# Key rope rotated on GpSimd, and the key-value latent turned ahead of the fourth query product, in a two-layer encoder

## What is computed

```python
def _mla(h, pos, w_in, g_q, g_kv, w_uq, w_ukv, w_o):
    lat = h @ w_in
    cq, ckv, k_rope = jnp.split(lat, [Q_LORA, Q_LORA + KV_LORA], axis=-1)      # 384, 256, 32
    cq = _rmsnorm(cq, g_q)
    ckv = _rmsnorm(ckv, g_kv)
    q = (cq @ w_uq).reshape(B, S, B_HEADS, NOPE_DIM + ROPE_DIM)                # 16 heads of 64 + 32
    kv = (ckv @ w_ukv).reshape(B, S, B_HEADS, NOPE_DIM + V_DIM)
    q_nope, q_rope = q[..., :NOPE_DIM], q[..., NOPE_DIM:]
    k_nope, v = kv[..., :NOPE_DIM], kv[..., NOPE_DIM:]
    q_rope = _rope(q_rope, pos)
    k_rope = _rope(k_rope[:, :, None, :], pos)                                 # one for all heads
    k = jnp.concatenate([k_nope, jnp.broadcast_to(k_rope, (B, S, B_HEADS, ROPE_DIM))], axis=-1)
    q = jnp.concatenate([q_nope, q_rope], axis=-1) * ((NOPE_DIM + ROPE_DIM) ** -0.5)
    # softmax(q k^T) v per head, then @ w_o
```

## Time and profile before

| what | us |
|---|---|
| median of 3 runs | 1159.46 |
| lowest and highest of them | 1159.24, 1159.5 |
| the profiled execution's own time | 1159.29 |
| its span, first to last instruction | 1157.5 |
| busy in the span: TensorE matmul / weight load | 1140.8 / 954.4 |
| busy: VectorE / GpSimd / ScalarE | 606.1 / 452.3 / 336.1 |

### The profile page before, as it was taken

How to read it: one execution, slowest core, us unless ns; L and a number is a source line. 1 busy time by engine, 2 the same in 40 slices (tenths; PEclk the granted TensorE clock), 3 DMA queues, 4 the chain that set the end, 5 groups by cost and what they waited for, 6 DMA issues and landing times.

```text
span 1157.5 us, 16884 instructions
## 1 busy us (share of the span) xinstructions
PE 1140.8 (99%) x5625; PEld 954.4 (82%) x5625; DVE 606.1 (52%) x1029; ACT 336.1 (29%) x705; POOL 452.3 (39%) x476
## 2 busy tenths in 40 slices
PE   7999999999999999999999999999999999999997
PEld 6877688888888888888988888888888888888886
DVE  5788864534424434455389888654434333334343
ACT  7387822111100111111277777522111000111102
POOL 3467753333311332334156445653233212333352
PEclk9999999999999999999999999999999999999999
DMA  7411123333432333333211001133333323333421
GB/s 192 110 38 37 37 74 91 102 97 91 118 100 73 96 104 91 111 101 97 84 39 40 19 19 37 37 110 91 94 105 97 107 86 91 91 107 92 125 75 73
DMA packets 177089, 97.80 MB, mean 84 GB/s; under 512 B 8848, under 2 KB 173200, under 8 KB 177040
## 3 DMA queue, kind: packets, MB, share of 16 engines
q1 hardware_dynamic: 177040, 97.17, 28.8%
HBM read 94.01 MB, written 2.10 MB: 83 GB/s over the span
## 4 chain that ended last, share of the span: by engine, by line
PE 94%; DVE 2%; ACT 1%; DMA 1%; POOL 1%; issue 1%; SPq 0%; ACTq 0%; DVEq 0%
PE bank L1365 28%; PE bank L1369 28%; PE bank L1368 28%; PE bank L1936 2%; PE bank L1955 1%; PE bank L1958 1%; PE bank L1526 1%; PE bank L1510 1%; PE bank L1882 1%; DMA gains<-in_norm_mix 1%; PE bank L1541 1%; PE bank L1542 1%; ACT s_a L957 0%; PE bank L1720 0%; DVE s_a L2288 0%
## 5 line engine op out<-in xcount | busy, mean ns | idle before, releaser
L2129 DVE TENSOR_TENSOR w_lo<-w_raw,w_hi 128x1024 fp32r<-128x1024 f32 (+3 forms) x139 | 189.1, 1361 | 280.7 <-POOL w_hi L510 280.6
L510 POOL TENSOR_SCALAR w_hi<-w_raw 128x1024 fp32r<-128x1024 f32 (+3 forms) x147 | 166.3, 1131 | 412.6 <-PE bank L1369 412.6
L1365 PE MATMUL bank<-x_hi,w_lo 128*128 128x512 f32 x760 | 297.1, 391 | 0.0
L1369 PE MATMUL bank<-x_hi,w_hi 128*128 128x512 f32 x760 | 295.8, 389 | 0.0
L1368 PE MATMUL bank<-x_lo,w_hi 128*128 128x512 f32 x760 | 295.8, 389 | 0.0
L1369 PEld LDWEIGHTS bank<-x_hi,w_hi 128*128 128x128 f32 x760 | 142.6, 188 | 29.7
L1368 PEld LDWEIGHTS bank<-x_lo,w_hi 128*128 128x128 f32 x760 | 142.7, 188 | 29.3
L1365 PEld LDWEIGHTS bank<-x_hi,w_lo 128*128 128x128 f32 x760 | 142.7, 188 | 29.2
L1365 PE MATMUL bank<-f_hi,w_lo 128*128 128x512 f32 (+1 forms) x363 | 139.7, 385 | 0.0
L1369 PE MATMUL bank<-f_hi,w_hi 128*128 128x512 f32 (+1 forms) x363 | 139.0, 383 | 0.0
L1368 PE MATMUL bank<-f_lo,w_hi 128*128 128x512 f32 (+1 forms) x363 | 138.9, 383 | 0.0
(11 more groups left out here) (276 smaller groups left out, 1868.1 us busy)
## 6 DMA issues: line engine op xcount, KB each, us to landing
w_raw<-in_ffn_w_gu SPq DMA_DIRECT2D x88, 512.0 KB, 3.8
w_raw<-in_ffn_w_down SPq DMA_DIRECT2D x32, 704.0 KB, 4.4
w_raw<-in_a_w_qkv SPq DMA_DIRECT2D x10, 512.0 KB, 3.8
w_raw<-in_a_w_o SPq DMA_DIRECT2D x8, 512.0 KB, 3.5
w_raw<-in_b_w_o SPq DMA_DIRECT2D x8, 512.0 KB, 3.6
w_raw<-in_b_w_in SPq DMA_DIRECT2D x4, 672.0 KB, 4.0
w_raw<-in_b_w_uq SPq DMA_DIRECT2D x4, 576.0 KB, 4.0
x_n<-in_x SPq DMA_DIRECT2D x4, 512.0 KB, 5.3
```

The costliest lines, as they stand in the source:

```text
L510: pool.tensor_scalar(split_part(w_hi, s, cols, kv), raw_part(s, cols, kv), 1.0, 1.0, ALU.mult, ALU.mult) \
L1365: first = pe.matmul(o, ll, rh, start=start, stop=False)
L1369: return pe.matmul(o, lh, rh, start=False, stop=stop)
L2129: dve.tensor_tensor(split_part(w_lo, s, cols, kv), raw_part(s, cols, kv), f(split_part(w_hi, s, cols, kv)), ALU.subtract) \
```

## The change

The rope columns of the latent are scaled and rotated by five GpSimd instructions, ahead of the scaling of the key-value latent, counted by a new semaphore `krope_rot`; VectorE's rotation of them is gone. GpSimd scales token tiles 0 and 1 of the key-value latent, VectorE tiles 2 and 3, ahead of its low part of the key-value weights. TensorE turns the key-value latent and the rope columns ahead of the fourth query product. ScalarE copies the fourth query result out behind the rope columns' copy. VectorE makes `ckv_lo` between the two query rotations. TensorE then makes the first key product ahead of the first query turn, and the first value product ahead of the third query turn; the mark moves to the key product. The counts of `rope_v` are four lower throughout.

```diff
             w_split_hi(C_B // 2, 1, W_UKV, kv=True)
 
+            pool.wait_ge(rs_n_ready, 3)
+            pool.wait_ge(lat_kv_ready, NT)
+            pool.wait_ge(kv_sq_ready, NT)
+            pool.wait_ge(tab_v, TAB_STEPS + 4)
+            krope = lat[:, :, QL + KVL:B_IN]
+            rope_x, rope_y = (r[:, 0:NT * ROPE].rearrange("p (t d) -> p t d", t=NT) for r in (rope_a, rope_b))
+            pool.tensor_tensor(krope, krope, rs_n[:, ::2].unsqueeze(2).to_broadcast([P, NT, ROPE]), ALU.mult) \
+                .then_inc(krope_rot, 1)
+            pool.wait_ge(krope_rot, 1)
+            pool.tensor_tensor(rope_x, krope, cos_n[:], ALU.mult).then_inc(krope_rot, 1)
+            pool.tensor_tensor(rope_y[:, :, 0:16], krope[:, :, 16:32], sin_n[:, :, 0:16], ALU.mult).then_inc(krope_rot, 1)
+            pool.tensor_tensor(rope_y[:, :, 16:32], krope[:, :, 0:16], sin_n[:, :, 16:32], ALU.mult).then_inc(krope_rot, 1)
+            pool.wait_ge(krope_rot, 4)
+            pool.tensor_tensor(krope, rope_x, rope_y, ALU.add).then_inc(krope_rot, 1)
+
             pool.wait_ge(lrs_step, LRS_KV)
-            for t in range(NT):
+            for t in range(2):
                 view = lat[:, t, QL:QL + KVL]
...
             act.wait_ge(lrs_step, LRS_Q)
-            for t in range(NT):
+            for t in range(NT - 1):
                 b_q_out(0, t)
...
             act.activation(krope_t[NOPE:QK, :], banks[0][0:ROPE, :], ACT.Copy).then_inc(krope_copied, 1)
+            b_q_out(0, NT - 1)
             act.wait_ge(krope_copied, 1)
...
                 if hd == 0:
-                    pe.wait_ge(rope_v, 8 * g + 12)
+                    pe.wait_ge(rope_v, 8 * g + 8)
...
             b_q(0, 2)
-            b_q(0, 3)
 
             pe.wait_ge(latn_ready, NT)
             pe.wait_ge(pt_free, T_BPRE + 6)
             for b in range(KVL // P):
                 lat_turn(lat_banks[6 + b], QL // P + b, range(NT))
-            pe.wait_ge(rope_v, 4)
+            pe.wait_ge(krope_rot, 5)
             pe.wait_ge(q_out_ready, 1)
...
             last.then_inc(krope_turned, 1)
+            b_q(0, 3)
...
-            b_turn_q(0, 0, mark=True)
-            b_k(0, 0)
+            b_k(0, 0, mark=True)
+            b_turn_q(0, 0)
             b_turn_q(0, 1)
+            b_v(0, 0)
             b_turn_q(0, 2)
-            b_v(0, 0)
             scores(0, 0)
...
             cq_low(1)
+            for t in range(2, NT):
+                view = lat[:, t, QL:QL + KVL]
+                dve.tensor_scalar(view, view, lat_stat[:, 2, NT + t:NT + t + 1], None, ALU.mult).then_inc(latn_ready, 1)
             w_split_lo(C_B // 2, 1, W_UKV, kv=True)
-
-            dve.wait_ge(rs_n_ready, 3)
-            krope = lat[:, :, QL + KVL:B_IN]
-            lrs(dve.tensor_tensor(krope, krope, rs_n[:, ::2].unsqueeze(2).to_broadcast([P, NT, ROPE]), ALU.mult))
             dve.wait_ge(tab_v, TAB_STEPS + 4)
-            rotate(krope, cos_n[:], sin_n[:],
-                   rope_a[:, 0:NT * ROPE].rearrange("p (t d) -> p t d", t=NT),
-                   rope_b[:, 0:NT * ROPE].rearrange("p (t d) -> p t d", t=NT), 0)
...
-            dve.wait_ge(rope_v, 4)
+            dve.wait_ge(krope_rot, 5)
             b_rotate_q(0, 0)
-            b_rotate_q(0, 1)
             for b in range(KVL // P):
                 b_pt_lo(T_BPRE + 6 + b, lat_banks[6 + b][:], ckv_lo[:, b, :], ckv_hi[:, b, :], g_kv[:, b:b + 1])
+            b_rotate_q(0, 1)
```

More of the change, by code:

```diff
@@ L332, in build @@
         rope_v = sem("rope_v")
+        krope_rot = sem("krope_rot")
         krope_turned = sem("krope_turned")
@@ L2710, in b_rotate_q @@
                        rope_a[:].rearrange("p (t h d) -> p t h d", t=NT, h=HG)[:, ts],
-                       rope_b[:].rearrange("p (t h d) -> p t h d", t=NT, h=HG)[:, ts], 8 * g + 4 * half + 4)
+                       rope_b[:].rearrange("p (t h d) -> p t h d", t=NT, h=HG)[:, ts], 8 * g + 4 * half)
             def b_k_lo(g, i):
```

## The result

| | before | changed kernel |
|---|---|---|
| median us | 1159.37 (7 runs, 1158.29 to 1161.28) | 1163.02 (7 runs, 1162.10 to 1163.84) |
| profiled execution, us / its span | 1159.29 / 1157.5 | 1162.10 / 1160.3 |
| ratio to before, 95% interval | | 1.0031, 1.0021 to 1.0040 |

The change makes the kernel slower by 3.65 us, 0.3%, outside the forecast range.

The account below looks back on a forecast made before the run. TensorE was taken as the bound, busy 1140.8 of 1157.5 us. With 0.5 lost on blocked norms and 0.4 gained behind, +0.1 us gave 1159.4 on the profiled scale, 1159.6 as a median; range 1158.5 to 1160.9.

Parts of the forecast that it names:

- The rest at nothing: Weight-slot marks, SP's next load and GpSimd's copies for heads 2 and 3: no cost; without cover, each below 1 us.
- the 0.5: Delay in us of TensorE from the third query product on, from VectorE's inverse norms blocked by GpSimd; bounds 0 to 1.3.
- norm chain: VectorE's tiny inverse-norm operations, ahead of cq_low: four with two SBUF inputs meet GpSimd's rope rotation, losing 0.5 us.
- rival 2: GpSimd's latent scaling caught behind VectorE's w_lo: +1.3 us in all, 1160.8; chance 0.15.
- Stake: TensorE's two waits before the first query turn and first key product: closing them gives at most 1.64 us.
- both gaps: TensorE's waits for the rotated queries, 0.9 us, and put down to "issue", 0.7 us; together 1.64 us.
- GpSimd's rotation: Five GpSimd operations on the latent's rope columns, from about 579.95: 2.04 us plus two semaphore steps of 0.1.
- VectorE's two scalings: VectorE scales two latent tiles behind cq_low: 0.3 us each, 0.6 for both, covered by the third query product.
- The gain behind it: Behind the norms, up to the first scores: new order brings them from 592.85 to 592.46, a gain of 0.4 us.
- the sum of 0.1: Whole change: 0.5 us lost on the blocked inverse norms, 0.4 gained behind them, +0.1 us in all.
- Rival 1: No blocking of VectorE's inverse norms by GpSimd: -0.4 us, 1159.1; chance 0.25.
- The text's own test: The forecast is wrong if a wait of over 1 us shows on TensorE elsewhere in the mixer.

Follow-up runs that it names:

- e1: The changed kernel, but GpSimd waits until the second query rotation is done before its rope rows of heads 2 and 3 and all behind them; 1158.82 us.
- e10: The changed kernel plus 28 unread transposes of the identity on TensorE behind the first key product, filling its wait for the second rotation; 1162.00 us.
- e3: The changed kernel, but only GpSimd's next weight rounding waits for the second query rotation; its two subtractions still run beside the rotation; 1161.21 us.
- e6: The kernel before the change plus four unread GpSimd additions, 128x256 with both inputs in SBUF, right behind its scaling of the latent; 1166.41 us.
- e2: The changed kernel, but GpSimd waits for the second query rotation behind its two rope-row roundings and ahead of its two subtractions; 1158.85 us.
- e7: The kernel before the change plus six unread GpSimd memsets of 128x512, which only write SBUF, behind its scaling of the latent; 1160.07 us.

## Why the prediction was wrong

**The step that failed** is the sentence in "The rest at nothing" on GpSimd's copies for heads 2 and 3: that they "get earlier", and that without cover each would cost below 1 us. They were priced as work that might be late, not as work that stands beside VectorE; so was the weight rounding behind them, whose mark the same paragraph moves. Counted from the start of the stretch, the rotation ran from 8.17 to 9.45 before (586.39 to 587.67, less 578.22), and the subtractions began at 10.92. The change moved the rotation to 9.58, because the fourth query product now comes behind the two turns on TensorE, and the subtractions to 9.69, because the rope rows are turned earlier. Both moves were in the forecast; that they meet was not. Its own terms place them together: the rotation at 587.55 and the 0.5, which is 9.83, and the subtractions, 1.57 earlier by the turn (584.65 instead of 586.22) and 0.5 later, at 9.85 (an estimate from its numbers). The forecast had even shown, with the earlier trace rows, what such a meeting does, and applied it only to the norm chain and, in rival 2, to the scaling of the latent. What the runs showed in place of "below 1 us": in e1, where the meeting is taken out by one wait, the stretch is 3.80 us shorter.

**The account of the loss.** Of the 3.80 us between e1 and the changed kernel, 3.05 are the rotation (4.34 less 1.29) and 0.73 the lower clock by e10. Less the 0.31 that e1 gains on before, the 3.80 leave the 3.49 seen.

**Point by point.**
- Stake: that both gaps hold only 1.64 us was right, and no version got more than 0.45 out of them. The chance for slower by over 0.2% was put at 0.04, and that is what came.
- GpSimd's rotation was forecast at 0.46 and 0.33 an operation; the first took 0.40, and the five lasted from 579.34 to 581.39, 2.05 us against 2.24 with the forecast's two steps of 0.1. Right.
- VectorE's two scalings: 0.6 forecast, 0.61 measured. GpSimd's two took 0.94 together and weren't caught behind `w_lo`; rival 2 didn't occur. TensorE turned the latent at 583.35 without a wait. Right.
- Norm chain: 0.5 forecast, 0.32 measured (the step from its first operation to `cq_lo` went from 1.55 to 1.87). The first of the four operations came 0.10 ahead of GpSimd and was free, at 0.17; the others took 0.32, 0.25 and 0.25. The mechanism was right, its size too large.
- The gain behind it was forecast at 0.4. In e1, without the collision, it is 0.63 (0.31 net and the 0.32). With the missed step out of the way, the sum of 0.1 would have been -0.1 with the norm chain as measured, and -0.3 with the gain as measured too; e1's stretch shows the -0.31, and its profiled execution, 1159.19, is 0.10 below that of the kernel before.
- Rival 1 (no blocking) was wrong where it was put: the chain was blocked. The text's own test, a wait of over 1 us elsewhere on TensorE, is the one that fired.

What stays open: why the medians of e3 and e6 lie further from the changed kernel and from before than their stretches do. It isn't time elsewhere in the traces: e6's profiled execution is 5.37 us above that of before, which is its stretch, 6.04 longer, less the 0.67 by which it began earlier; the other three executions of e6, not profiled, took 1.6 to 2.2 us more.

## What to carry to other kernels

When an edit shifts work between engines, list for each stretch which two-input VectorE operations and which SBUF-reading GpSimd operations will stand side by side in the new order, not only which is late: a VectorE operation of 0.28 us then costs the whole of a GpSimd operation of 1.3 us, and again for each next pair. Work of GpSimd that nobody waits for soon, such as rope rows of heads 2 and 3, deserves a wait that keeps it off VectorE's critical operations: here one `wait_ge` brought the stretch from 18.12 to 14.32 us and the median from 1163.02 to 1158.82. Where a wait of TensorE grows, look at the granted clock behind it too: it was at 0.50 behind the waits of 2.27 us (e3) and 3.15 us (changed kernel).

## What the runs showed of the hardware

- Two engines that each have a queue of such operations take turns, one for one: four GpSimd additions of 0.73 to 0.79 us (e6; 0.734 in the earlier trace rows) held four VectorE operations for about 0.5 us each, and GpSimd's own four took 3.28 in all with the waits for their semaphores.
- A GpSimd subtraction on 32 partitions by 512 takes as long as one on 128: 1.28 where it stood beside no blocking operation (both in e1), against 1.277. The few partitions of the rope rows make it no cheaper, and it blocked VectorE for nearly its whole length (1.37 and 1.34 beside 1.46 and 1.30).
- The last part of a GpSimd operation blocked nothing: the rotation's first operation began at 587.04, 0.14 before the end of the roundings (585.98 and 1.20), and took its usual 0.42; e2 and e3 show the same.
- It goes both ways: in e3 the weight rounding, begun 0.05 us behind a VectorE subtraction with two SBUF inputs, took 1.64 instead of 1.15.
- GpSimd's memsets (six in 3.44 us, e7) held up no VectorE operation.
- An idle time of 3.15 us on TensorE was followed by about 3 us at a granted clock of 0.50, worth 0.73 us here; with transposes in the gap (e10) the clock stayed at 1.00.
